# Order of the softmax steps, the gate chunk and the score products in the attention heads of a two-block fp32 kernel

## The reference, cut to what matters

```python
q = (_rmsnorm(cq, q_norm[l]) @ w_q_b[l]).reshape(B, S, N_HEADS, QK_HEAD_DIM)      # 128 + 64 per head
q_nope, q_rope = q[..., :QK_NOPE_DIM], _apply_rope(q[..., QK_NOPE_DIM:], cos_q, sin_q)
kv = (_rmsnorm(ckv, kv_norm[l]) @ w_kv_b[l]).reshape(B, S, N_HEADS, QK_NOPE_DIM + V_HEAD_DIM)
k_nope, v = kv[..., :QK_NOPE_DIM], kv[..., QK_NOPE_DIM:]
s = (jnp.einsum("bqhd,bkhd->bhqk", qn_b, k_nope)
     + jnp.einsum("bqhr,bkr->bhqk", qr_b, k_rope)).astype(jnp.float32) * scale
p = jax.nn.softmax(s, axis=-1).astype(v.dtype)
y_a = jnp.einsum("bhqk,bkhd->bqhd", p, v) * jax.nn.silu(z_a)                      # z_a = h @ w_in[..]
y = jnp.concatenate([y_f, y_a], axis=-1) @ w_out[l]
```

## Time and profile before

| | |
|---|---|
| median of 3 runs | 2088.84 us (2087.76 to 2093.28) |
| the profiled execution | 2092.68 us, its span 2091.0 us |
| TensorE busy, VectorE busy, ScalarE busy | 97%, 67%, 44% of the span |
| heads of layer 0 | about 258 to 372 us of the span |
| heads of layer 1 | about 646 to 751 us |

### The profile page before, as it was taken

The page is one execution under the profiler, slowest core; times in us unless marked ns, Lnnn a source line. Parts: engine busy times, 40 slices in busy tenths (PEclk is TensorE's granted clock), DMA queues, the critical chain, the costliest instruction groups (busy, mean ns, idle before and its releaser), DMA issues.

```text
span 2091.0 us, 34367 instructions
## 1 busy us (share of the span) xinstructions
PE 2025.8 (97%) x13117; PEld 1793.1 (86%) x13117; DVE 1404.2 (67%) x1943; ACT 920.8 (44%) x1364; POOL 35.2 (2%) x69
## 2 busy tenths in 40 slices
PE   5999998999999899999999999999999999999998
PEld 2789887779998888999999999888888888888886
DVE  5358877786687667888997555566456546645655
ACT  2344445454645444433346334454334434434543
POOL 0000000000000000000000000000000000000000
PEclk9999999999999999999999999999999999999999
DMA  9988778865576664344544555545555555555553
GB/s 363 392 342 320 297 262 327 327 249 203 200 267 240 251 232 181 142 171 174 180 179 176 207 181 182 220 148 194 190 192 181 200 188 194 182 199 183 190 191 139
DMA packets 64982, 462.05 MB, mean 221 GB/s; under 512 B 7328, under 2 KB 7872, under 8 KB 9328
## 3 DMA queue, kind: packets, MB, share of 16 engines
q1 hardware_dynamic: 56288, 399.61, 51.8%
q0 software_dynamic: 8592, 61.00, 7.8%
HBM read 458.45 MB, written 2.13 MB: 220 GB/s over the span
## 4 chain that ended last, share of the span: by engine, by line
PE 70%; DVE 6%; ACT 1%; issue 0%; DVEq 0%; ACTq 0%
PE ps L605 17%; PE ps L606 17%; PE ps L607 17%; PE ps L622 11%; PE ps L623 6%; DVE w_lo L1860 2%; PE ps L653 0%; ACT sc L1566 0%; DVE area L1897 0%; DVE X L2401 0%; DVE y_lo L1880 0%; PE ps L1047 0%; DVE grow L2502 0%; DVE area L2502 0%; DVE csil L2342 0%
## 5 line engine op out<-in xcount | busy, mean ns | idle before, releaser
L1860 DVE TENSOR_TENSOR w_lo<-raw,w_hi 128x1024 fp32r<-128x1024 f32 (+2 forms) x650 | 750.5, 1185 | 371.5 <-ACT w_hi L1299 370.3
L1299 ACT CAST w_hi<-raw 128x1024 fp32r<-128x1024 f32 (+3 forms) x650 | 637.9, 1021 | 459.7 <-PE ps L607 451.4
L605 PE MATMUL ps<-a,w_lo 128*128 128x256 f32 (+1 forms) x1888 | 540.6, 286 | 6.7 <-DVE sc L2134 3.7
L606 PE MATMUL ps<-a,w_hi 128*128 128x256 f32 (+1 forms) x1888 | 534.8, 283 | 0.0
L607 PE MATMUL ps<-a,w_hi 128*128 128x256 f32 (+1 forms) x1888 | 534.0, 283 | 0.0
L605 PEld LDWEIGHTS ps<-a,w_lo 128*128 128x128 f32 x1888 | 357.5, 189 | 31.7 <-issue 22.8
L622 PE MATMUL ps<-a,w_hi 128*128 128x512 f32 x1024 | 358.7, 393 | 0.4 <-DVE a L1982 0.4
L607 PEld LDWEIGHTS ps<-a,w_hi 128*128 128x128 f32 x1888 | 357.5, 189 | 0.0
L606 PEld LDWEIGHTS ps<-a,w_hi 128*128 128x128 f32 x1888 | 356.3, 189 | 0.5 <-issue 0.5
L623 PE MATMUL ps<-a,w_lo 128*128 128x256 f32 x1024 | 287.1, 280 | 0.0
L605 PE MATMUL ps<-w_hi,y_lo 128*128 128x512 f32 x720 | 281.2, 391 | 0.0
(11 more groups left out here) (307 smaller groups left out, 2224.6 us busy)
## 6 DMA issues: line engine op xcount, KB each, us to landing
raw<-in_stream SPq DMA_DIRECT2D x328, 1024.0 KB, 4.8
area<-in_ada POOLq DMA_DIRECT2D x50, 1024.0 KB, 5.3
area<-in_ada SPq DMA_DIRECT2D x38, 1024.0 KB, 8.2
grow<-in_ada SPq DMA_DIRECT2D x8, 1024.0 KB, 8.2
area<-in_rows POOLq DMA_DIRECT2D x4, 1024.0 KB, 4.9
raw<-in_stream SPq DMA_DIRECT2D x7, 384.0 KB, 5.2
X<-in_x SPq DMA_DIRECT2D x1, 2048.0 KB, 9.6
grow<-row_scratch POOLq DMA_DIRECT2D x2, 1024.0 KB, 7.1
```

What stands on the lines that cost most here:

```text
L605: pe.matmul(o, w[1], a[0], start=first, stop=False, skip_group_check=shared)
L606: pe.matmul(o, w[0], a[1], start=False, stop=False, skip_group_check=shared)
L1299: ac.copy(to, raw[:, bass.ds((g % RAW) * CH + at, n)]).then_inc(hi_ready, 1)
L1860: ve.tensor_tensor(to, raw[:, bass.ds((g % RAW) * CH + at, n)], hi.bitcast(F32), ALU.subtract).then_inc(lo_ready, 1)
```

## The change

It has no other work than before, in another order. (1) VectorE: the maximum stands directly behind `turned(h - 1)`, ahead of `y_tile` and `gate`; the two halves of the next gate chunk stand one ahead of `y_tile` and one behind `gate`; `turned` stands behind the projection chunk's halves and the added step. (2) TensorE: the turn of the probabilities stands behind 12 of the 16 gate blocks. (3) The two 128-row score products come first, then the two 64-row ones. (4) ScalarE: `y_part` behind the exponentials. (5) Ahead of the heads: the second rotation behind `y_first(7)` and `y_rest(7)`, `project(0)` into bank 4. (6) `finish_rows(3)` behind the last head's scores.

```diff
                     half(g, 0)
                     if first:
+                        pe.wait_ge(v_l, 4 * l + 2)
+                    if h == 1:
                         pe.wait_ge(qr_rot, 2 * (l + 1))
...
-                    blocks(par, bank(0), lat, range(QT), True, True)
+                    blocks(par, bank(qk_bank(h)), lat, range(QT), True, True)
...
                 def turn_queries():
 
+                    pe.wait_ge(qr_rot, 2 * (l + 1))
                     pe.wait_ge(v_l, 4 * l + 3)
...
                     blocks(par, bank(2), a_ops, range(8), True, False)
-                    if l == 0 and h == HEADS - 1:
-                        finish_rows(3)
-                    if not first:
+                    half(g + 1, 1)
+                    blocks(par, bank(2), a_ops, range(8, 12), False, False)
+                    if first:
+                        turn_queries()
+                    else:
                         turn(h - 1)
...
+                    blocks(par, bank(2), a_ops, range(12, 16), False, True).then_inc(weights_used, 1)
...
                         mm3(bank(5, qt * T), (qk_hi[:, s], qk_lo[:, s]), (qk_hi[:, T:2 * T], qk_lo[:, T:2 * T]),
-                            True, False)
+                            qt == 0, False, True)
+                    for qt in range(2):
+                        s = slice(qt * P, (qt + 1) * P)
                         o = mm3(bank(5, qt * T), (qr[0][:, s], qr[1][:, s]), (kr_hi[of_pair, :], kr_lo[of_pair, :]),
-                                False, True)
+                                False, qt == 1, True)
...
+                    if l == 0 and h == HEADS - 1:
+                        finish_rows(3)
...
-                    if not first:
-                        y_part(GROUPS + h - 1)
                     ac.wait_ge(s_max, 8 * l + h + 1)
                     for qt in range(2):
                         ac.activation(sc[:, qt * T:(qt + 1) * T], bank(5, qt * T), ACT.Exp,
                                       bias=stat[:, 2 + qt:3 + qt], scale=SM_SCALE,
                                       accum_out=stat[:, 4 + qt:5 + qt]).then_inc(s_exp, 1)
+                    if not first:
+                        y_part(GROUPS + h - 1)
...
                     if not first:
+                        turned(h - 1)
+                    ve.wait_ge(s_ps, 8 * l + h + 1)
+                    own.link(ve.tensor_reduce(stat[:, 0:2], bank(5, 0, 2 * T).rearrange("p (q k) -> p q k", q=2),
+                                              AX.X, ALU.max))
+                    ve.tensor_scalar(stat[:, 2:4], stat[:, 0:2], -SM_SCALE, None, ALU.mult).then_inc(s_max, 1)
+                    split(g + 3, slot_of(g0 + 1), halves=(0,))
+                    if not first:
                         ve.wait_ge(o_ps, 8 * l + h)
                         ve.wait_ge(z_ready, 16 * l + GROUPS + h)
                         y_tile(GROUPS + h - 1, bank(4))
                         ve.wait_ge(y_mul, 16 * l + GROUPS + h)
                     gate(GROUPS + h, bank(2))
...
+                    split(g + 3, slot_of(g0 + 1), halves=(1,))
+                    if not first:
                         y_rest(GROUPS + h - 1)
```

More of the change, by code:

```diff
@@ L359, in qr_pairs, with qk_bank @@
             return free_columns(w_hi), free_columns(w_lo)
+        def qk_bank(h):
+            return 0 if h else 4
         def qr_bank(i):
@@ L1026, in lat @@
                         return lat_hi[:, k * T:(k + 1) * T], lat_lo[:, k * T:(k + 1) * T]
[L1027 removed]
+                    blocks(par, bank(qk_bank(h)), lat, range(QT), True, True)
                     half(g, 1)
                     for k in range(QT, QT + CT):
[L1030 removed]
+                        o = mm3(bank(qk_bank(h), T), wb(par, k), lat(k), k == QT, k == QT + CT - 1)
                     o.then_inc(weights_used, 1)
                 def turn_queries():
+                    pe.wait_ge(qr_rot, 2 * (l + 1))
                     pe.wait_ge(v_l, 4 * l + 3)
@@ L1072, in head @@
                     blocks(par, bank(2), a_ops, range(8), True, False)
-                    if l == 0 and h == HEADS - 1:
-                        finish_rows(3)
-                    if not first:
-                        turn(h - 1)
-                    half(g + 1, 1)
-                    if first:
-                        blocks(par, bank(2), a_ops, range(8, 12), False, False)
-                        turn_queries()
-                        blocks(par, bank(2), a_ops, range(12, 16), False, True).then_inc(weights_used, 1)
-                    else:
-                        blocks(par, bank(2), a_ops, range(8, 16), False, True).then_inc(weights_used, 1)
+                    half(g + 1, 1)
[3 more added lines that the diff above has]
+                    else:
+                        turn(h - 1)
+                    blocks(par, bank(2), a_ops, range(12, 16), False, True).then_inc(weights_used, 1)
                     pe.wait_ge(q_l, 8 * l + h + 1)
@@ L1545, in head @@
                     ac.wait_ge(weights_used, g + 1)
-                    ac.copy(qk_hi, bank(0, 0, 2 * T)).then_inc(q_h, 1)
+                    ac.copy(qk_hi, bank(qk_bank(h), 0, 2 * T)).then_inc(q_h, 1)
                     after(g, g0)
@@ L2269, in rotate @@
                     r = ROPE // 2
-                    if tt:
-                        ve.wait_ge(qr_rot, 2 * l + 1)
-                    else:
-                        ve.wait_ge(y_l, 16 * l + GROUPS - 1)
+                    ve.wait_ge(y_l, 16 * l + GROUPS - 1 + tt)
                     ve.tensor_tensor(to, q, cos.to_broadcast([P, HEADS, ROPE]), ALU.mult)
@@ L2295, in _ @@
                 after(G + L_QR, G + L_QR)
-                values(0)
-                rotate(1)
-                for i in (1, 2, 3):
-                    values(i)
-                after(G + L_V, G + L_V)
-                ve.wait_ge(qr_rot, 2 * (l + 1))
-                y_first(GROUPS - 1)
-                y_rest(GROUPS - 1)
+                for i in range(4):
+                    values(i)
+                split(G + L_HEAD + 1, slot_of(L_HEAD + 1), halves=(0,))
+                ve.wait_ge(qr_rot, 2 * l + 1)
+                y_first(GROUPS - 1)
+                split(G + L_HEAD + 1, slot_of(L_HEAD + 1), halves=(1,))
+                y_rest(GROUPS - 1)
+                rotate(1)
                 def turned(h):
@@ L2312, in head @@
                     ve.wait_ge(q_h, 8 * l + h + 1)
-                    sub_hi(qk_lo, bank(0, 0, 2 * T), qk_hi).then_inc(q_l, 1)
+                    sub_hi(qk_lo, bank(qk_bank(h), 0, 2 * T), qk_hi).then_inc(q_l, 1)
                     if l:
@@ L2316, in head @@
                     split(g + 2, slot_of(g0), halves=(0,))
-                    if not first:
-                        turned(h - 1)
                     if first:
@@ L2335, in head @@
                     gate(GROUPS + h, bank(2))
-                    if h < HEADS - 1:
-                        after(g + 1, g0 + 1)
-                        if not first:
-                            y_rest(GROUPS + h - 1)
-                    ve.wait_ge(s_ps, 8 * l + h + 1)
-                    own.link(ve.tensor_reduce(stat[:, 0:2], bank(5, 0, 2 * T).rearrange("p (q k) -> p q k", q=2),
-                                              AX.X, ALU.max))
-                    ve.tensor_scalar(stat[:, 2:4], stat[:, 0:2], -SM_SCALE, None, ALU.mult).then_inc(s_max, 1)
-                    if h == HEADS - 1:
-                        after(g + 1, g0 + 1)
+                    split(g + 3, slot_of(g0 + 1), halves=(1,))
+                    if not first:
                         y_rest(GROUPS + h - 1)
```

1 line of the change is left out of this document (removed).

## The result

The changed kernel takes 2060.55 us (median of four, 2058.90 to 2063.81), the kernel before 2089.64 beside it (2087.76 to 2093.28). The ratio is 0.9861, with a 95% interval of 0.9841 to 0.9880: faster, by 29.1 us. The forecast was 2060 us.

The account below looks back on a forecast made before the run. TensorE, busy 97% of the span, was taken as the bound. Gains 17.6 + 2.8 + 6.3 + 4.0 + 1.4 = 32.1, less 0.9 and 1.4, give 29.8 us: 2059.0 from the 2088.84 median, stated as 2060, range 2053 to 2071.

Parts of the forecast that it names:

- The maximum's place: VectorE in each head: the earlier maximum, not the turn's later place, brings most of the turn's 17.6 us.
- The 17.6 us: TensorE's 12 waits at the turn for ScalarE's multiplications, 15.8 us plus 12 x 0.15 of overlap, all go.
- the 2.8 of `finish_rows(3)`: Last head of layer 0: TensorE's 2.73 us wait for a modulation step, 2.8 with overlap, goes.
- 0.20 us for each change of rows: Scores: each change between 128-row and 64-row products costs 0.20 us; two fewer a head, 16 heads, save 6.3 us.
- Ahead of the heads: First gate chunk of each layer: its 2.0 us wait for `y_first(7)` goes, 4.0 us in all.
- Layer 1's first scores: Start of layer 1's heads: the wait for low parts of queries grows to 1.7 us, a loss of 0.9.
- Head 0: First head of each layer: late `gate` costs 1.0 us in layer 0 and 0.45 in layer 1, together 1.4.
- The tie behind the other heads: Gate chunk waiting for `gate` behind the early maximum: ready S + 3.3, wanted S + 3.2; taken as 0.
- The clock term: Layer 0, behind the first gate chunk's wait: 15 matmuls at the low clock go with that wait, 1.4 us.
- The loads in layer 0: Rival, heads 2 to 6: loads bind at 384 GB/s wanted, losing 1.5 to 10 us, giving 2066; chance 0.12.
- ready 1.2 + 0.7 us behind the turn's start: `pt_lo` in each head: ready then and wanted 3.6 us behind the turn's start, so the later turn costs nothing.
- VectorE as the bound: Rival: VectorE's 11.2 us list in layer 0 makes TensorE wait, 7 to 14 us, 2066 to 2073; chance 0.18.

Follow-up runs that it names:

- e2: Changed kernel with the turn of the probabilities back behind 8 of the 16 gate blocks: 2061.85 us.
- e3: Changed kernel with maximum, next gate chunk's halves and `y_part` in their old places, turn left behind 12 blocks, `pt_lo` behind the modulation step: 2080.51 us.
- e9: Changed kernel with VectorE's and ScalarE's lists in a head as before, `pt_lo` ahead of the modulation step, turn still behind 12 blocks: 2072.84 us.
- e8: Changed kernel with maximum, halves and `y_part` in their old places and the turn behind 8 blocks, `pt_lo` behind the modulation step: 2083.20 us.
- e1: Changed kernel with the score products in the old order, 128 then 64 rows for each half of the queries: 2063.69 us.
- e7: Kernel before with the new order of the score products alone: 2086.79 us, ratio 0.9984.
- e4: Changed kernel with the stage ahead of the heads as before (rotation, two halves, then `y_first(7)`) and `project(0)` in its old bank: 2064.71 us.
- e5: Changed kernel with the loads of the modulation rows that TensorE adds cut to a quarter of their columns: 2058.99 us.
- e10: Changed kernel with the turn back behind 8 blocks and, in layer 0, `pt_lo` ahead of the modulation step: 2060.77 us.

## Why the prediction was right, and where it wasn't

- **The maximum's place carries the turn's gain: right.** The 17.6 us went, and so did the 2.8 of `finish_rows(3)`, which no longer waits. e2 shows that the turn's move gave nothing, e3 and e9 that without the early maximum 20 and 12 us are missing (the 20 with `pt_lo` behind the step, the 12 with it ahead). The chain came out close to its working: maximum at S + 0.31 (0.3), `gate` done at S + 3.12 (3.2), reciprocal at S + 4.5 (4.7), a head of layer 1 10.92 us (11.0). What the prediction left out is that the turn's move alone would have been worth up to some 10 us (e9 against e8) had the maximum stayed: two cures for one wait, of which the second adds nothing once the first is in.
- **0.20 us for each change of rows: right in size, for layer 1.** 0.41 a head in e1, 0.37 to 0.40 in e7. The step that failed is "16 heads: 6.3 us": in layer 0 the shorter head only brought the wait for loads nearer (e1), so some 3 us remain.
- **Ahead of the heads: right.** From the start of the stage to the first scores layer 0 went from 26.90 to 23.30, 3.6 us. Layer 1's first scores lose 1.88 (2.00 from start to start, less 0.12), where the forecast, counted in the same way, had 1.7.
- **Head 0: close.** TensorE loses 0.82 us to `gate` in layer 0 (0.94 from start to start, less 0.12) and 0.36 in layer 1 (0.48 less 0.12), where 1.0 and 0.45 were taken. The tie behind the other heads costs 0.08 in layer 1 (0.20 less 0.12) and nothing in heads with an added row.
- **The clock term: wrong as a cause.** "Nothing else stood still there" tied the low clock to the wait of the first gate chunk. The stretch there is gone, but one like it stands at 324 us, behind the wait of 1.31; and e4 has the old wait back without a fall of the clock. In the traced execution the 1.4 us were moved, not removed, and that the clock fell once in both traces is luck for the total.
- **The loads in layer 0: the chance was mis-sized.** The rival had 0.12 and came true, in the lower half of its 1.5 to 10 us: 4.2 (e5). Its working compared GB/s: 384 wanted, 415 seen elsewhere. The failing piece was that comparison: the 415 are of a stretch with other loads, while in these heads 383 to 404 GB/s took a share of 0.97 to 1.00 of the DMA engines (e1, its three stretches from 294 to 336), and heads of 11.8 us want 329 x 14.0 / 11.8 = 390. Little of the 7% to spare was there. The rate alone doesn't tell which kernel waits, though: e1 moved 388 GB/s over 290 to 336 us with no wait of TensorE where the changed kernel moved 376 with them. A second reading, argued from rows, is one slot of `area` going round: step 2.35, some 0.3 until the next load is issued, its landing, and the next step. The rows of the changed kernel's POOL, the issue for the slot whose step started at 308.38, and of e1, for the one that started at 303.86 (with that step's row):

```profile
298.35 0.53 POOL L534 DMA_DIRECT2D area<-in_ada  x1 [4.59 <-DVE area L1903]
```

```profile
294.63 0.53 POOL L534 DMA_DIRECT2D area<-in_ada  x1 [3.58 <-DVE area L1901]
...
303.86 2.35 DVE L1901 SCALAR_TENSOR_TENSOR area<-area,csil 128x2048 f32<-128x2048 f32 x1
```

  From issue to step it is 10.0 us in the changed kernel, with a wait, and 9.2 in e1, without one. Going round takes 2.65 + 10.0 = 12.7 us, more than the head's 11.8. The kernel before left 11.3 us for it (13.95 less 2.65) and never waited. Had the prediction set a landing (8.4 us in the kernel before, median) against 11.8 less 2.65 = 9.1 us of room, it would have seen how near that is. That the loads into `grow` on SP's queue stretch the landing is shown by e5. It takes bytes off each head as well, so no run separates full DMA engines from a slot's round; that the loads are the cause is shown, which limit of theirs is not. The prediction's "ready 1.2 + 0.7 us behind the turn's start" also left out the modulation step that stands ahead of `pt_lo`: in the head whose `attend` starts at 324.52 `pt_lo` ended 5.8 us behind the turn's start (318.62 to 324.46). The Trainium skill, page "DMA: Bandwidth & Descriptors", section Specifications, has about 358 GB/s as the HBM limit of a NeuronCore; heads at 370 to 375 and, in e1, 14 us at 391 are above it, so the trace decides against that number here too, though not against the rival.
- **VectorE as the bound: did not come true** by itself. Without late loads (e5) no `attend` of layer 0 waits for it, and a gate chunk waits more than 0.1 us only behind head 0, as the sum had it.
- **Why the total fits all the same.** Layer 1: 12.8 against 12.9. Layer 0: 16.9 less the 4.2 that e5's trace puts on loads and clock gives 12.7, and 14.6 were measured; the 1.9 are the heads' surplus, since in e5 a head of layer 0 gains 13.95 less 11.76 = 2.19 us where the sum had 1.9 (the 0.11 in the gate chunk, which was set against a tie, and 0.06 behind the turn are most of it). The last 1.4 us came from the start of the program, where TensorE waited 2.4 us less for loads in this execution; between kernels of this study that wait was 13.0 to 19.3 us, so it is scatter. A right total hid an error of 4 us in layer 0, offset by a surplus of 1.9 there and by the scatter: that part of the fit is luck.

## What to carry to other kernels

A wait at a consumer is cured where its chain begins: the early maximum made the move of the consumer worthless, while moving the consumer without it had at most some 10 of the 22.7 us and passed the rest of the lateness to the next one (e3, e9). Where loads go through a ring, take the highest GB/s from a stretch with the same mix of loads (here 383 to 404, where 415 had been seen elsewhere), and compare a slot's round (use, issue, landing) with the new period of the loop as well. And a saving of TensorE counts only in the stages where TensorE's own work is what sets the period: the same 0.4 us a head was worth 2.7 us in layer 1 and nothing in layer 0 (e1).

## What the runs showed of the hardware

- A wait of TensorE of 1.3 to 3 us is followed by up to some 3.3 us of matmuls 0.21 instead of 0.12 apart (granted clock 0.53 to 0.62, 1.2 GHz for the most part) in some executions and not in others: behind the 1.84 us wait of layer 0 in the kernel before, but not behind the same wait of layer 1 (1.85), nor behind either in e4 (1.86 and 1.85); behind 1.31 us in layer 0 of the changed kernel, but not behind 1.73 in its layer 1; behind 2.70 ahead of the turn in the last head of layer 0 in e7, but not behind the 2.73 at that place in the kernel before. The clearest case is the wait of 1.72 to 1.73 us ahead of layer 1's first scores, the same in eight kernels: the clock fell behind it in e2, e9 and e10 and not in the changed kernel, e1, e3, e5 and e8. So the length of the wait alone doesn't decide it; what does stays open. One such stretch costs 1.0 (the stage of e2 and e10) to 1.4 us.
- A 1 MB load into `area` from POOL's queue lands in 8.4 us (median) beside SP's loads in the kernel before at 331 GB/s, 9.1 in the changed one at 372 GB/s, and 6.0 in e5 at 352 GB/s (stretch 294 to 336 us of each). With the loads beside it cut to a quarter, 5% less traffic brought a third off the landing.
- Between a 128-row and a 64-row product of 256 columns TensorE loses 0.20 us (distances of 0.21 and 0.23 us where 0.12 is usual), in both directions and in both orders of the scores, whether another product of the scores, `attend` or the next projection follows.
